# 88 instead of 80 tokens by index in a PEER trunk: sets of 64 and 24 tokens, scores and choice begun inside the query projection, a third of v in full fp32

## The chip, the cores and the metric

The kernel runs on 1 core of one Trainium2 chip. The metric is the device time of one execution in microseconds (us); one launch computes the whole output. Five engines work side by side: TensorE (PE, matmuls; its weight loads are listed apart as PEld), VectorE (DVE), ScalarE (ACT), GpSimd (POOL) and SyncE (SP), which issues most transfers; 16 DMA engines carry the transfers of all of them.

## The reference, cut to what matters

256 tokens of width 1024 go through two layers. Layer 0 mixes tokens with a convolution module, layer 1 with latent attention; after each comes a PEER block, in which every token reads 128 of 16384 experts.

```python
def peer(x, w_q, sub_keys, u, v):                      # x: 256 tokens x 1024
    q = (xt @ w_q).reshape(T, 8 heads, 2, 128)
    s = jnp.einsum('thpd,pnd->thpn', q, sub_keys)      # 128 scores, 2 sides, 8 heads
    sv, si = lax.top_k(s, 16)
    cand = sv[:, :, 0, :, None] + sv[:, :, 1, None, :]
    cv, ci = lax.top_k(cand.reshape(T, 8, 256), 16)
    experts = i1 * 128 + i2                            # 8 heads x 16 = 128 a token
    gates = jax.nn.softmax(cv)
    a = gelu(einsum('td,tkd->tk', x, u[experts])) * gates
    y = einsum('tk,tkd->td', a, v[experts])
# x = LayerNorm(alpha * x + mixer(x)), then x = LayerNorm(alpha * x + peer(x)), twice
```

u and v have 16384 rows of 4 KB each in fp32, for each layer.

## The kernel before

**Two ways through the experts.** The first DT = 176 tokens go by columns: TensorE multiplies them with all of u, in 128 blocks of 128 experts (512 KB each), ScalarE applies gelu, the result is multiplied with a sparse matrix of gates, and a second pass multiplies it with all of v, again in 128 blocks. The other SIDE = 80 tokens go by index: GpSimd fetches just their chosen rows of u and v by indirect DMAs (`gather`), one row of 4 KB to each partition, and VectorE does the sums over them (`side_dot` for u, `side_weighted` for v), 1024 elements on 128 partitions each time. The tokens by index come in sets, `SETS = ((64, 2), (16, 8))`: 64 tokens with 2 groups of partitions (64 of their rows a group), and 16 tokens with 8 groups (16 rows). That is 64 + 16 = 80 gathers of 512 KB for u and 80 for v in each layer. They have 5 rooms (`SIDE_BUFS`); gather n waits until VectorE has used the rows of n - 5 (`side_used`).

**Blocks.** SyncE loads the blocks of all weights in a fixed order into 4 rooms, and 3 more (`EXTRA`) while u and v are read; the next load waits for the room. A block is multiplied in one of two ways. *In full* (the set `FULL`): fp32 weights against fp32 tokens, which needs no other engine. *Split*: ScalarE rounds the block to fp32r (`make_high`), VectorE makes the rest (`make_low`, 1024 elements), and TensorE does 8 wide matmuls (rounded weights against both parts of the tokens side by side, 2 x DT columns) and 8 narrow ones (the rest of the weights, DT columns). In the profile a matmul in full has two records.

**Order of a layer's PEER part.** The query projection (`wq`, 16 blocks: 4 leading ones by rows, then 12 with `project_wide`; VectorE adds up the two products, `queryT`). Block 0 of u. The scores: 64 matmuls of 128 columns (32 instructions, 8 groups of four into 4 banks), copied by ScalarE. Then u's blocks up to `EARLY` = 37 without any gate, while VectorE makes the choice (`select`): 16 pairs of `top16` over the scores, 8 pairs over the candidates, then the decoding. Ahead of block `CHOSEN_AT` = 33 TensorE waits for `chosen_ok`, transposes the choice, and VectorE copies the choice of the tokens by index (`own_picks`), whereupon GpSimd starts to gather. The rest of u runs in 45 pairs of blocks (`project_merged`, `FULL_PAIRS` says which are in full); after 22 of them (`PAIR_OF`) a batch of 8 tokens is spread over the experts (`spread`, `make_onehots`, `scale_onehots`, `gate`), and `DOT_PAIRS` says which `side_dot` stands in which pair. After u come 120 blocks of v by columns (`combine_columns`; every fourth one in full, `FULL_V`), with `side_weighted` at the blocks of `SIDE_SUMS_AT` (block 4 to 113), and 8 last blocks by rows (`combine_tail`).

VectorE's order within a pair of u is: sum of the cross products, low of a coming block, the dots of `DOT_PAIRS`, the product with the gates that frees the banks (`late`), one-hots, another low, `scale_onehots`, `gate`. TensorE's next pair but one waits for `late`.

Of the kernel before, what the change touches and what calls it, by code (L numbers as in the profile page):

```python
# [14 lines left out]
P = 128  # L15
# [55 lines left out]
SET_ROWS = [PH * TOPK // _groups for _, _groups in SETS]  # L71
# [10 lines left out]
FULL_PAIRS = {1, 3, 5, 13, 21, 29, *PAIR_OF}  # L82
# [12 lines left out]
assert len(BATCH_OF) == BATCHES and len(SIDE_SUMS_AT) == SIDE_ROWS  # L95

# [32 lines left out]
FULL_V = [_n for _n in range(FIRST_COLUMNS, COLUMNS - LAST_COLUMNS) if _n % 4 == 3]  # L129
# [160 lines left out]
def program(nc, x_rows, x_cols, positions, conv_par, diag, mla_par, ln_par, keys, w_uq, w_uk, w_uv,  # L290
            u_rows, blocks, out):
    with ExitStack() as ctx:
# [213 lines left out]
        side_used = sem("side_rows_used")  # L506
        side_gelu = sem("side_hidden_made")
# [118 lines left out]
        def _(pool):  # L626
# [7 lines left out]
            nc.gpsimd.memset(rms_eps, RMS_EPS)  # L634
            nc.gpsimd.memset(ones[:], 1.0).then_inc(consts, 1)
# [23 lines left out]
            for layer in range(DEPTH):  # L659
# [5 lines left out]
                pool.wait_ge(own_picked, layer + 1)  # L665

                def fetch_picks(i, g):
                    n, rows, end_row = SETS[i][0], SET_ROWS[i], SET_ENDS[i]
                    half, at = divmod(rows * g, P // 2)
                    nc.gpsimd.dma_start(  # L670
                        picks[n * g:n * (g + 1), :, end_row - rows:end_row],
                        own_picks[SET_AT[i]:SET_AT[i] + n, :, half, at:at + rows]).then_inc(picks_in[i], 16)
# [9 lines left out]
                pool.wait_ge(picks_in[0], 16 * SETS[0][1] * (layer + 1))  # L682

                def gather(n):
                    if layer or n >= SIDE_BUFS:
                        pool.wait_ge(side_used, 2 * SIDE_ROWS * layer + max(0, n - SIDE_BUFS + 1))
                    rows, at = (u_rows, n) if n < SIDE_ROWS else (v_rows, n - SIDE_ROWS)
                    nc.gpsimd.indirect_dma_start(  # L688
                        out=side_rows[n % SIDE_BUFS], out_offset=None, in_=rows,
                        in_offset=bass.IndirectOffsetOnAxis(ap=pick_ids[:, at:at + 1], axis=0),  # L690
                        element_offset=layer * NKEYS * NKEYS * D
                    ).then_inc(side_in[n % SIDE_BUFS], 16)
                for n in range(2 * SIDE_ROWS):
# [6 lines left out]
                    elif i == 2 * groups:  # L700
                        pool.wait_ge(picks_in[1], 16 * groups * (layer + 1))
                        nc.gpsimd.memset(xT[:, :, :, DT:T].bitcast(F32), 0.0).then_inc(side_zero, 1)
# [12 lines left out]
        def _(pe):  # L715
# [180 lines left out]
            def add_sides(m):  # L896

                for pick, total in zip(selector, side_sum):
                    nc.tensor.matmul(y[:, 2 + m, :], pick, total[:, m * 512:(m + 1) * 512],  # L899
# [1457 lines left out]
```

## Time and profile before

| | |
|---|---|
| time, median of 3 runs | 1588.6 us (1587.27 to 1590.02) |
| the profiled execution: its time, its span | 1586.46 us, 1584.7 us |
| granted TensorE clock, mean | 0.998 |
| busy, share of the span | PE 98%, PEld 95%, DVE 84%, ACT 38%, POOL 38% |
| moved by DMA | 493.95 MB, mean 312 GB/s |
| layer 0: last query block ends, choice transposed, first block of v | 164.93, 250.87, 501.75 us |
| layer 1: the same | 939.75, 1025.53, 1276.83 us |

A row of a timeline is: start, length, engine, line, operation, out<-in, shape, count, and in brackets how long the engine sat idle before and what ended that. A row of windows is: stretch, its length, then for each engine the busy time and (x) instructions, the granted clock, the mean busy share of the 16 DMA engines, and GB/s moved.

### The profile page before, as it was taken

What the parts mean: (1) busy time and instruction counts of PE and PEld (TensorE: products, weight loads), DVE (VectorE), ACT (ScalarE), POOL (GpSimd) and SP (SyncE); (2) the same over time, 40 slices, a digit from 0 to 9 for tenths busy, and PEclk for the clock granted to TensorE, in tenths of its full rate; (3) what the DMA queues carried; (4) which work ended last, traced back from release to release, by engine and by line L of the source; (5) the groups of instructions that cost most, each with busy time, mean ns of one, the idle gap of its engine ahead of it and who ended that gap; (6) DMA issues with size and microseconds to landing.
All of it is one profiled execution on the core that took longest, in us unless ns stands there. A gap on an engine that the chain in (4) does not pass through costs nothing. (4 is left out here: it accounts for less than half of the span.)

```text
span 1584.7 us, 27912 instructions
## 1 busy us (share of the span) xinstructions
PE 1553.7 (98%) x10766; PEld 1497.9 (95%) x10766; DVE 1326.6 (84%) x2531; ACT 606.7 (38%) x1127; POOL 604.2 (38%) x438
## 2 busy tenths in 40 slices
PE   8999999999999999999999999999999999999998
PEld 8988999989999999999888899999999999999996
DVE  6986697889998998888856749958999988888895
ACT  5564221323234444544535341112333344444452
POOL 5651002654442555454003200046445435555420
PEclk9999999999999999999999999999999999999999
DMA  7644578999999999999823237799999999999990
GB/s 250 229 136 152 185 222 293 386 384 392 388 381 382 373 403 408 406 405 406 304 110 120 79 122 263 222 361 372 404 385 390 365 379 399 408 404 404 402 366 28
DMA packets 136964, 493.95 MB, mean 312 GB/s; under 512 B 16064, under 2 KB 16576, under 8 KB 136576
## 3 DMA queue, kind: packets, MB, share of 16 engines
q1 hardware_dynamic: 85248, 307.42, 52.4%
q0 software_dynamic: 47552, 170.06, 27.8%
q10 hardware_dynamic: 4032, 14.68, 2.6%
q8 instruction: 86, 1.41, 0.4%
q14 instruction: 46, 0.38, 0.1%
HBM read 488.79 MB, written 1.05 MB: 309 GB/s over the span
## 5 line engine op out<-in xcount | busy, mean ns | idle before, releaser
L688 POOL DMA_INDIRECT big<-v,picks x160 | 261.8, 1636 | 260.9 <-DVE big L1926 207.1
L688 POOL DMA_INDIRECT big<-u_rows,picks x160 | 214.9, 1343 | 227.6 <-DVE big L1842 193.9
L726 PE MATMUL work<-columns,raw 128*128 128x176 f32 x1728 | 268.0, 313 | 1.4 <-DVE big L1820 1.4
L726 PEld LDWEIGHTS work<-columns,raw 128*128 128x128 f32 x1728 | 259.4, 190 | 1.6 <-issue 1.6
L622 DVE TENSOR_TENSOR low<-raw,high 128x1024 fp32r<-128x1024 f32 x168 | 210.7, 1257 | 40.3 <-ACT high L1247 40.1
L1247 ACT ACTIVATE high<-raw 128x1024 fp32r<-128x1024 f32 x184 | 191.8, 1046 | 47.6 <-PE work L726 22.8
L726 PE MATMUL work<-columns,extra_raw 128*128 128x176 f32 x1280 | 202.0, 315 | 3.4 <-DVE big L1820 3.4
L1842 DVE SCALAR_TENSOR_TENSOR big<-big 128x1024 f32<-128x1024 f32 x160 | 190.2, 1218 | 15.0 <-DMA big<-u_rows,picks 15.0
L1926 DVE SCALAR_TENSOR_TENSOR big<-big,side_hid 128x1024 f32<-128x1024 f32 x156 | 199.6, 1280 | 2.3
L726 PEld LDWEIGHTS work<-columns,extra_raw 128*128 128x128 f32 x1280 | 193.5, 191 | 3.8 <-issue 3.8
L1508 ACT ACTIVATE xT<-big 128x176 fp32r<-128x176 f32 x198 | 67.6, 349 | 273.1 <-PE work L871 210.1
L866 PE MATMUL y<-xT,high 128*128 128x352 f32 x600 | 131.1, 340 | 2.4 <-DVE xT L1897 2.4
L866 PE MATMUL work<-xT,high 128*128 128x352 f32 x600 | 123.0, 326 | 0.0
L746 PE MATMUL work<-xT,high 128*128 128x352 f32 x544 | 102.8, 331 | 8.8 <-DVE big L1820 8.7
L622 DVE TENSOR_TENSOR low<-extra_raw,high 128x1024 fp32r<-128x1024 f32 x81 | 98.7, 1221 | 12.1 <-ACT high L1247 12.1
L670 POOL DMA_DIRECT2D picks<-beside_xT x20 | 12.0, 602 | 241.6 <-DVE beside_xT L1854 241.6
L866 PEld LDWEIGHTS work<-xT,high 128*128 128x128 f32 x600 | 101.0, 188 | 0.0
L866 PEld LDWEIGHTS y<-xT,high 128*128 128x128 f32 x600 | 95.9, 190 | 3.0 <-issue 3.0
L746 PEld LDWEIGHTS work<-xT,high 128*128 128x128 f32 x544 | 86.4, 188 | 11.2 <-issue 10.8
L871 PE MATMUL work<-xT,low 128*128 128x176 f32 x600 | 91.2, 274 | 0.0
L1247 ACT ACTIVATE high<-extra_raw 128x1024 fp32r<-128x1024 f32 x81 | 84.6, 1045 | 13.6 <-PE work L726 12.0
L871 PE MATMUL y<-xT,low 128*128 128x176 f32 x600 | 87.1, 267 | 0.0
(262 smaller groups left out, 2833.3 us busy)
## 6 DMA issues: line engine op xcount, KB each, us to landing
raw<-u SPq DMA_DIRECT2D x150, 512.0 KB, 6.7
raw<-v SPq DMA_DIRECT2D x146, 512.0 KB, 7.2
extra_raw<-v SPq DMA_DIRECT2D x110, 512.0 KB, 7.3
extra_raw<-u SPq DMA_DIRECT2D x106, 512.0 KB, 6.1
raw<-wq SPq DMA_DIRECT2D x32, 512.0 KB, 3.7
raw<-conv_in SPq DMA_DIRECT2D x14, 512.0 KB, 4.6
aux<-ln_par ACTq DMA_DIRECT2D x9, 512.0 KB, 9.1
raw<-conv_out SPq DMA_DIRECT2D x8, 512.0 KB, 4.0
```

What stands on the lines that cost most here:

```text
L622: ops.tensor_tensor(low_at(c), raw_at(c), high_at(c).bitcast(F32), ALU.subtract).then_inc(low_made[RAW_SLOT[c]], 1)
L670: nc.gpsimd.dma_start(picks[n * g:n * (g + 1), :, end_row - rows:end_row], own_picks[SET_AT[i]:SET_AT[i] + n, :, half, at:at + rows]).then ...
L688: nc.gpsimd.indirect_dma_start(out=side_rows[n % SIDE_BUFS], out_offset=None, in_=rows, in_offset=bass.IndirectOffsetOnAxis(ap=pick_ids[:, ...
L726: mm = nc.tensor.matmul(out_, raw_at(c)[:, k * P:(k + 1) * P], x_full[:, k, :], start=(k == 0), stop=(k == KD - 1))
L746: nc.tensor.matmul(both, w_high[:, cols], xT[:, k, :, 0:DT], start=(k == 0), stop=False)
L866: nc.tensor.matmul(columns_bank(k), high_at(c)[:, k * P:(k + 1) * P], xT[:, slot, :, 0:DT], start=start, stop=False)
L871: return nc.tensor.matmul(columns_bank(k)[:, 0, :], low_at(c)[:, k * P:(k + 1) * P], xT_high[:, slot, 0:DT], start=False, stop=stop)
L1247: A(high_at(c), raw_at(c), ACT.Copy).then_inc(high_made, 1)
L1508: A(xT_high[:, (c - v0) % KD, 0:DT], hid[:, c - v0, :], ACT.Copy).then_inc(a_high, 1)
L1842: V.scalar_tensor_tensor(rows, rows, 1.0, side_x[set_of(d)], ALU.mult, ALU.mult, accum_out=side_hid[:, d:d + 1]).then_inc(side_used, 1)
L1926: V.scalar_tensor_tensor(total, rows, weight, total, ALU.mult, ALU.add).then_inc(side_used, 1)
```

## The change

88 tokens go by index instead of 80, so 168 instead of 176 by columns. The second set has 24 tokens with 5 groups of 26 rows: 120 partitions are used, and 5 x 26 = 130 places hold 128 rows, so the picks and the hidden values are cleared once. There are 64 + 26 = 90 gathers for u and for v instead of 80; 26 of each 90 are of 120 rows. The rooms for them become 6. Six of the eight groups of score matmuls move into the query projection (after its blocks 2, 6 and 10), and VectorE takes the top 16 of six pairs there. `EARLY` goes from 37 to 29, `CHOSEN_AT` from 33 to 27; there are 49 pairs (28 in full, 21 split, before 28 and 17) and 21 batches. Of v 38 blocks instead of 29 are in full.

```diff
-EARLY = 37
+EARLY = 29
-CHOSEN_AT = 33
-EXP_AT = 24
+CHOSEN_AT = 27
+EXP_AT = 21
+SCORES_AT = (2, 6, 10)
+TOPS_AT = {4: 0, 6: 1, 8: 2, 9: 3, 10: 4, 11: 5}
-SETS = ((64, 2), (16, 8))
+SETS = ((64, 2), (24, 5))
-SET_ROWS = [PH * TOPK // _groups for _, _groups in SETS]
+SET_ROWS = [-(-PH * TOPK // _groups) for _, _groups in SETS]
+SET_USED = [_n * _groups for _n, _groups in SETS]
-FULL_PAIRS = {1, 3, 5, 13, 21, 29, *PAIR_OF}
+FULL_PAIRS = {7, 15, 21, 28, 35, 42, 47, *PAIR_OF}
-FULL_V = [_n for _n in range(FIRST_COLUMNS, COLUMNS - LAST_COLUMNS) if _n % 4 == 3]
+FULL_V = [_n for _n in range(FIRST_COLUMNS, COLUMNS - LAST_COLUMNS) if _n % 3 == 1]
...
                 def gather(n):
...
                     rows, at = (u_rows, n) if n < SIDE_ROWS else (v_rows, n - SIDE_ROWS)
+                    used = SET_USED[set_of(at)]
                     nc.gpsimd.indirect_dma_start(
-                        out=side_rows[n % SIDE_BUFS], out_offset=None, in_=rows,
-                        in_offset=bass.IndirectOffsetOnAxis(ap=pick_ids[:, at:at + 1], axis=0),
+                        out=side_rows[n % SIDE_BUFS][0:used], out_offset=None, in_=rows,
+                        in_offset=bass.IndirectOffsetOnAxis(ap=pick_ids[0:used, at:at + 1], axis=0),
...
-                for c in range(FIRST[wq] + LEAD[wq] + HALVES, end_of[wq]):
+                full = FIRST[wq] + LEAD[wq]
+                for c in range(full + HALVES, end_of[wq]):
                     project_wide(wq, c)
+                    if c - full == SCORES_AT[0]:
+                        pe.wait_ge(lead_ok, HALVES * (layer + 1))
+                        pe.wait_ge(keys_in, 16 * (layer + 1))
+                        make_scores(0, 2)
+                    elif c - full == SCORES_AT[1]:
+                        pe.wait_ge(emptied, PROJECTED[wq] + 4)
+                        make_scores(2, 4)
+                    elif c - full == SCORES_AT[2]:
+                        pe.wait_ge(emptied, PROJECTED[wq] + 8)
+                        make_scores(4, 6)
...
                 pe.wait_ge(emptied, PROJECTED[f"u{layer}"])
...
+                make_scores(6, 8)
                 project(f"u{layer}", 1, CHOSEN_AT)
...
+            def top_pair(layer, pair):
+
+                n = pair // 2
+                j = HP * (n % HALVES) + 4 * (n // HALVES) + 2 * (pair % 2)
+                dve.wait_ge(score_ok, 8 * layer + n + 1)
+                top16([(j + lane, scores[:, j + lane, :], rest[lane]) for lane in range(2)], top_v, top_u)
+
             def select(layer):
 
-                dve.wait_ge(score_ok, 8 * (layer + 1))
...
+                for pair in range(len(TOPS_AT), HP):
+                    top_pair(layer, pair)
...
                     make_low(dve, V, c + RING)
+                    if c - full in TOPS_AT:
+                        top_pair(layer, TOPS_AT[c - full])
                 select(layer)
```

**TensorE, from the last query blocks to the transposed choice.** `work<-xT` with 512 columns is a wide query matmul, `y<-big 128x128` a score matmul, `work<-columns` a block of u in full (x8 is one block), `y<-ident,aux` the choice transposed. Before:

```order
L807 MATMUL work<-xT,high 128x512 x8
L810 MATMUL work<-xT,low 128x256 x8
L726 MATMUL work<-columns,raw 128x176 x8
L1154 MATMUL y<-big 128x128 x32
L726 MATMUL work<-columns,raw 128x176 x24
```

and the same place in the changed kernel:

```order
L826 MATMUL work<-xT,high 128x512 x8
L829 MATMUL work<-xT,low 128x256 x8
L1167 MATMUL y<-big 128x128 x8
L826 MATMUL work<-xT,high 128x512 x8
L829 MATMUL work<-xT,low 128x256 x8
L745 MATMUL work<-columns,raw 128x168 x8
L1167 MATMUL y<-big 128x128 x8
L745 MATMUL work<-columns,raw 128x168 x24
```

Of the 32 score matmuls 24 have moved ahead of u, in three pieces of 8, the last of which is the first `y<-big` shown here; 8 stay behind u's block 0.

**GpSimd, the gathers of layer 0.** `big<-u_rows,picks` and `big<-v,picks` are gathers of u and of v, `picks<-beside_xT` brings a part of the choice. Before, from the last piece of the second set's tokens on:

```order
L676 DMA big<-x 16x1024
L688 DMA big<-u_rows,picks 128x1024
L702 MEMSET xT 128x16x80
L688 DMA big<-u_rows,picks 128x1024 x55
L688 DMA big<-v,picks 128x1024 x80
```

and in the changed kernel:

```order
L694 DMA big<-x 24x1024
L707 DMA big<-u_rows,picks 128x1024
L721 MEMSET xT 128x16x88
L707 DMA big<-u_rows,picks 128x1024 x45
L707 DMA big<-u_rows,picks 120x1024 x26
L707 DMA big<-v,picks 128x1024 x64
L707 DMA big<-v,picks 120x1024 x26
```

The second set's gathers are of 120 rows now, and there are 26 of them instead of 16, for u and for v.

## Rows read from the trace of the kernel before

**Rows 1.** The page, busy times and bandwidth in 40 slices
```profile
PE 1553.7 (98%) x10766; PEld 1497.9 (95%) x10766; DVE 1326.6 (84%) x2531; ACT 606.7 (38%) x1127; POOL 604.2 (38%) x438
...
GB/s 250 229 136 152 185 222 293 386 384 392 388 381 382 373 403 408 406 405 406 304 110 120 79 122 263 222 361 372 404 385 390 365 379 399 408 404 404 402 366 28
```

**Rows 2.** Windows: the stretches of gathers, and parts of the first
```profile
257.50:755.30 497.80, 490.41 (x3638) 487.40 (x3637) 442.15 (x597) 189.94 (x343) 248.30 (x177) 1.00 1.01 391
300.00:340.00 40.00, 37.00 (x282) 36.22 (x282) 33.63 (x53) 12.40 (x26) 26.29 (x26) 1.00 1.03 376
340.00:360.00 20.00, 19.91 (x158) 19.66 (x158) 19.93 (x30) 6.31 (x13) 10.04 (x7) 1.00 1.03 406
...
580.00:600.00 20.00, 20.00 (x145) 20.00 (x145) 19.01 (x24) 9.01 (x15) 10.97 (x7) 1.00 1.03 409
...
1033.00:1528.00 495.00, 488.27 (x3616) 485.75 (x3616) 433.55 (x574) 186.30 (x337) 248.63 (x177) 1.00 1.01 391
```

**Rows 3.** DMA issues: KB each, us from issue to landing
```profile
raw<-v SPq DMA_DIRECT2D x146, 512.0 KB, 7.2
...
raw<-wq SPq DMA_DIRECT2D x32, 512.0 KB, 3.7
...
big<-u_rows,picks POOLq DMA_INDIRECT x160, 8.4
```

**Rows 4.** Timeline of PE: blocks of u, in full and split
```profile
486.72 2.55 PE L726 MATMUL work<-columns,raw 128*128 128x176 f32 x16
489.10 1.06 PE L1181 MATMUL y<-aux 128*128 128x128 f16 x16
490.02 1.54 PE L746 MATMUL work<-xT,high 128*128 128x352 f32 x8
491.40 1.03 PE L749 MATMUL work<-xT,low 128*128 128x176 f32 x8
492.26 1.50 PE L746 MATMUL work<-xT,high 128*128 128x352 f32 x8
```

**Rows 5.** Timeline of PE: blocks of v, one round of four
```profile
508.90 1.39 PE L879 MATMUL y<-big,extra_raw 128*128 128x176 f32 x8
...
515.68 0.84 PE L866 MATMUL y<-xT,high 128*128 128x352 f32 x4
...
517.87 1.39 PE L879 MATMUL y<-big,extra_raw 128*128 128x176 f32 x8
```

**Rows 6.** Timeline of PE: last query block to the transposed choice
```profile
162.13 2.00 PE L807 MATMUL work<-xT,high 128*128 128x512 f32 x8
...
164.93 2.55 PE L726 MATMUL work<-columns,raw 128*128 128x176 f32 x16
167.32 7.31 PE L1154 MATMUL y<-big 128*128 128x128 f32 x64
174.46 7.33 PE L726 MATMUL work<-columns,raw 128*128 128x176 f32 x48
...
250.87 0.88 PE L1165 MATMUL y<-ident,aux 128*128 128x128 f32 x6
```

**Rows 7.** Timeline of DVE: last query sum, first pairs of the choice
```profile
165.54 0.42 DVE L2221 TENSOR_TENSOR big<-work,cross 128x256 f32<-128x256 f32 x1 [2.37 <-ACT cross L1478]
175.29 0.49 DVE L1698 MAX8 big<-big 128x8 f32<-128x128 f32 x2 [9.32 <-ACT big L1484]
...
177.65 0.47 DVE L1698 MAX8 big<-big 128x8 f32<-128x128 f32 x2
```

**Rows 8.** Timeline of POOL: the first gather of layer 0
```profile
257.47 1.17 POOL L688 DMA_INDIRECT big<-u_rows,picks  x1 [3.39 <-DMA picks<-beside_xT]
```

**Rows 9.** Groups of DVE by line, 256 to 502 us
```profile
L1842 DVE SCALAR_TENSOR_TENSOR big<-big 128x1024 f32<-128x1024 f32 x80 | 95.0, 1218 | 7.2 <-DMA big<-u_rows,picks 7.2
...
L622 DVE TENSOR_TENSOR low<-raw,high 128x1024 fp32r<-128x1024 f32 x22 | 26.8, 1219 | 4.3 <-ACT high L1247 4.3
...
L1820 DVE TENSOR_TENSOR big<-work,big 128x16 f32<-128x16 f32 (+21 forms) x44 | 15.1, 344 | 14.6 <-ACT work L1498 14.6
```

More of the change, by code:

```diff
@@ L95, with pick_pieces @@
 assert len(BATCH_OF) == BATCHES and len(SIDE_SUMS_AT) == SIDE_ROWS
+def pick_pieces(i, g):
+    lo, hi = SET_ROWS[i] * g, min(SET_ROWS[i] * (g + 1), PH * TOPK)
+    return [(a, b) for a, b in ((lo, min(hi, P // 2)), (max(lo, P // 2), hi)) if a < b]
+PICK_LOADS = [sum(len(pick_pieces(_i, _g)) for _g in range(SETS[_i][1])) for _i in range(len(SETS))]
 def set_of(d):
@@ L506, in program @@
         side_used = sem("side_rows_used")
+        side_filled = sem("side_tables_zeroed")
         side_gelu = sem("side_hidden_made")
@@ L681, in _ @@
                     fetch_tokens(0, g)
-                pool.wait_ge(picks_in[0], 16 * SETS[0][1] * (layer + 1))
+                pool.wait_ge(picks_in[0], 16 * PICK_LOADS[0] * (layer + 1))
                 def gather(n):
@@ L700, in _ @@
                     elif i == 2 * groups:
-                        pool.wait_ge(picks_in[1], 16 * groups * (layer + 1))
+                        pool.wait_ge(picks_in[1], 16 * PICK_LOADS[1] * (layer + 1))
                         nc.gpsimd.memset(xT[:, :, :, DT:T].bitcast(F32), 0.0).then_inc(side_zero, 1)
@@ L896, in add_sides @@
             def add_sides(m):
-                for pick, total in zip(selector, side_sum):
-                    nc.tensor.matmul(y[:, 2 + m, :], pick, total[:, m * 512:(m + 1) * 512],
+                for pick, total, used in zip(selector, side_sum, SET_USED):
+                    nc.tensor.matmul(y[:, 2 + m, :], pick[0:used], total[0:used, m * 512:(m + 1) * 512],
                                      start=False, stop=False)
@@ L1471, in _, with copy_scores @@
                         highs_to(full + RING)
+                def copy_scores(lo, hi):
+                    for n in range(lo, hi):
+                        at = HP * (n % HALVES) + 4 * (n // HALVES)
+                        act.wait_ge(score_mm, 8 * layer + n + 1)
+                        A(scores[:, at:at + 4, :].rearrange("p j n -> p (j n)"), y[:, n % 4, :],
+                          ACT.Copy).then_inc(score_ok, 1)
                 for c in range(full, end_of[wq]):
@@ L1479, in _ @@
                     highs_to(c + RING)
+                    if n - 1 in SCORES_AT:
+                        copy_scores(2 * SCORES_AT.index(n - 1), 2 * SCORES_AT.index(n - 1) + 2)
                 u0 = FIRST[f"u{layer}"]
-                for n in range(HALVES * HP // 4):
-                    act.wait_ge(score_mm, 8 * layer + n + 1)
-                    A(scores[:, 4 * n:4 * n + 4, :].rearrange("p j n -> p (j n)"), y[:, n % 4, :],
-                      ACT.Copy).then_inc(score_ok, 1)
+                copy_scores(6, 8)
                 def gelu(n):
```

80 lines of the change are left out of this document (42 added, 38 removed).

## The prediction

> **What bounds the kernel now.** First the page: TensorE is busy for 98% of the span, and nearly the same slices that hold u and v move 380 to 408 GB/s and never more [rows 1]. So there are two candidates, TensorE and the DMA engines, and I looked at whether either has room. From the first gather of layer 0 (257.5 us) to the 113th block of v (755.3 us) TensorE works for 490.4 of 497.8 us, so it waits for 7.4 us, at the full clock; VectorE works for 442 of them; and the DMA engines have a mean busy share of 1.01 while they move 391 GB/s. Layer 1 repeats it: 391 GB/s over 495 us [rows 2]. A share of 1.01 means that each of the 16 engines has a packet under way all the time. The pieces of that stretch show where it tops out: 409 GB/s from 580 to 600 us, 406 from 340 to 360, and 376 from 300 to 340, where the small pieces of the choice are moved too, all with a share of 1.03 [rows 2]. A load of a block takes 3.7 us alone and 7.2 us in this stretch, a gather 8.4 [rows 3]: they queue. So TensorE sets the pace today, with the DMA engines at 391 of some 404 GB/s right behind it: 3% of room. VectorE is the third: in u it carries 80 dots of 1.19 us (95.0 / 80), and TensorE's few stalls come through its line L1820, which waited 14.6 us for gelus [rows 9].
>
> The chance of a gain lies where TensorE sets the pace; a change that asks for more bytes in less time must pass the other limit.
>
> **What TensorE saves.** A block of u in full starts 2.38 us before what follows (486.72 to 489.10), a split one takes 2.24 us: 1.38 us for 8 wide matmuls and 0.86 for 8 narrow ones; a batch's spread takes 0.92 [rows 4]. In v one round of four blocks takes 8.97 us, a split block in it 2.19 (515.68 to 517.87) [rows 5]. A block in full has 16 records of 176 columns in 2.38 us, 149 ns each, which is 2 x 176 columns at 2.4 GHz (147 ns) and 2 ns; with 168 columns it is 142 ns or 2.28 us. A wide matmul loses 16 columns, 6.7 ns, so a split block 0.05 us. The narrow ones take 108 ns at 176 columns where the columns alone would be 73; something else sets that, so I take nothing for them (at most 8 x 3.3 ns, 0.03 us). In v a third in full makes a round of three 2.28 + 2 x 2.15 = 6.58 us, 2.19 a block instead of 2.24.
>
> After the choice u has before 61 blocks in full, 34 split and 22 spreads: 145.2 + 76.2 + 20.2 = 241.6 us, and took 250.9 (250.87 to 501.75 in the table). After the change: 59 in full, 42 split, 21 spreads: 134.5 + 92.0 + 19.3 = 245.8. To block 113 of v: 113 x 2.24 = 253.1 before, 247.5 after. TensorE alone would thus need 493 us from the choice on, where it took 504.
>
> **When the choice comes.** Before, the last query block ends at 164.93, u's block 0 and 7.14 us of scores follow (167.32 to 174.46), then 32 blocks; TensorE arrives at 250.87 and waits for nothing [rows 6]. VectorE starts its first pair at 175.29, after 9.32 us of idling, and needs 2.36 us a pair [rows 7], so 16 pairs last to 212.9; the rest (to 250.8) is 37.9. After: six of eight groups of scores, 5.4 us, lie in the projection, which then ends at 170.3. A block takes 2.80 us there (162.13 to 164.93 [rows 6]), and VectorE has 0.42 for its sum [rows 7] and 1.22 for a low [rows 9]; three pairs stand at blocks with a low, where it falls behind by about 1.2 us and catches up at the next block without a pair; the other three at blocks without one. So I cost these at nothing; if TensorE did wait there, it would be 1.2 us at each of three places. The last sum ends at 171.3, pair 5 and ten more follow without a pause: 25.9, then 37.9: 235.1. TensorE gets there at 170.3 + 27 x 2.28 + 1.8 = 233.7 and waits 1 us or so. The choice comes at 234.9, 16.0 us earlier. The first gather keeps its distance (257.47, 6.6 us behind the transposition [rows 8]), and 6 more blocks of u are yet to be loaded and multiplied.
>
> **VectorE in u.** 10 more dots (11.9 us), 8 more lows (9.8), 4 more cross sums and products with gates (some 3), one batch less (3.3): about 21 us more on top of the roughly 218 it works between 256 and 502 us. That is 239 in a stretch of some 255; it is near the limit but does not exceed what the transfers need (below). In v 10 more sums of 1.28 stand against 9 lows and 9 small operations less: nothing.
>
> **What the DMA engines must carry.** The stretch of rows 2 moved 497.8 us x 391 GB/s = 194.6 MB, that is 371 transfers of 512 KB. The change adds: 20 gathers, of which 52 of now 180 are 120 / 128 of a whole: 16.75 transfers; 6 blocks that were there already when gathers started: 6. It takes away the lead that blocks have at the end: with 7 rooms at 2.24 us a block a room comes round every 15.7 us, of which 7.2 is the load [rows 3] and 2.2 the multiplication, so about 3 blocks lie ready; in a stretch that the transfers limit they are used up: -3. The sum is +19.75 transfers, 10.4 MB, 205.0 MB in all. What rate? The low bound is that of before over the whole stretch, 391; the high bound is 409 everywhere. With work queued all the time the idle moments go, while the small pieces of the choice (376 for 40 us) stay; a stretch of 40 us at 376 and the rest at 404 to 409 is 404 to 406. I take 402, since VectorE near its limit will leave some gaps. 205.0 / 0.402 = 510 us, 12 more than before; less 16.0 for the earlier choice: -4 us a layer. TensorE's 493 us, 6.6 of it before the first gather, are hidden under these 510 + 6.6.
>
> Outside of this stretch the change touches 7 blocks of v (0.3 us) and two clears of GpSimd at the start: nothing. Two layers: -8 us. The profiled execution's 1586.5 us becomes 1578.5 (its span 1584.7 becomes 1577); it lies 2.1 us under the median of the runs, so the forecast is 1581 us.
>
> Where that turns: the rate at which the longer list takes exactly 497.8 + 16.0 us is 399 GB/s. Above, the change is faster, below, slower. At 391 it is 524 us: +10.5 a layer. At 406 it is 505: -9.
>
> One price is not in the trace: a gather of 120 rows. From the rows it costs between 120/128 of a whole one (taken) and a whole one, if the engines that hold most rows set its end: 52 / 16 = 3.25 transfers more, +4.2 us a layer, and the forecast becomes no change. The Trainium skill (DMA: Bandwidth & Descriptors, section Queues, rings and completion order) says that a transfer is split over the largest number of engines up to 16 that divides the partitions, 15 for 120, taken in turn, and that some direct copies by GpSimd put the partitions divided by 16, rounded up, on each engine, which would be 8 on each of the first 15. By the first way the smaller price holds, by the second the larger; no run so far shows which.
>
> **The rivals.**
>
> *TensorE keeps the pace.* If the engines could carry what is asked, each layer would take 16.0 us less up to the choice and 504 - 493 = 11 less behind it, or 2 less if the same stalls stay: -18 to -27 a layer, 1535 to 1553 us, middle 1544. For it: TensorE's 98%. Against it: v would ask for a block each 2.19 us and a gather each 1.233 blocks, 524 KB x (1 / 2.19 + 1 / 2.70) = 433 GB/s, and no window with a share of 1.03 is above 409 [rows 2]. The same page (section Specifications) gives a ceiling of 435 GB/s for the core's ports. By that rule this rival holds, and the time is its 1544 us; the trace, at 409 with every engine busy, speaks against it. Chance 0.12.
>
> *The transfers take more than they give.* The stretch keeps its rate of 391, since bursts of gathers and full rooms leave the same gaps, or VectorE's 239 us of work and late gathers hold each other up in u: +10.5 us a layer, 1610 us; with whole-price gathers up to 1618. It decides from under 399 GB/s. For it: the stretches of both layers had a share of 1.01 already and still only 391. Against: the 7.4 us in which TensorE waited show that before it was not the transfers that were asked for all they could. Chance 0.28, its smaller sizes (1592 up) included.
>
> *It cancels.* 399 GB/s, or 402 with gathers at the whole price: 1585 to 1592 us. Chance 0.18.
>
> My forecast, the transfers set the pace at 400 to 406 GB/s, 1568 to 1585 us, has 0.42.
>
> **The numbers.** The likeliest alone spans 1568 to 1585. The range must take in the cancelling and most of the slower case: 1558 to 1607; about 0.1 is left out on each side. A change of up to 0.2% (3.2 us) is about what a measurement of this kernel can't tell from none. Faster than that: 0.12 and 0.40 of the forecast's case, 0.52. Within: 0.17. Slower: 0.31.
>
> **What the changed profile would show.** DMA at a share of 1.03 and 400 to 409 GB/s all through both stretches; TensorE's records in full at 142 ns; TensorE busy for clearly less than 98% there, with waits that end at lows of late blocks or at gathers, in v too, where it had none; loads of v landing after more than 7.2 us. The choice transposed near 235 us. If TensorE works without gaps in v at 2.19 us a block, I am wrong about the ceiling; if the rate stays near 391 with gaps in the share, the slower case holds; if the choice comes later than 236 us, VectorE was held up in the projection. First block of v near 492 to 496 us in layer 0.

## The result and the profile after

The changed kernel takes 1734.3 us (median of 4 runs, 1731.8 to 1739.8) where the kernel before takes 1588.8 beside it: a ratio of 1.0922 (95% interval 1.0907 to 1.0937), 145.5 us slower. The forecast was 1581, and the slowest rival ended at 1618. The profiled execution of the changed kernel took 1733.2 us, its span is 1731.4.

First the page of the changed kernel, the lines that answer to [rows 1] and the chain of waits with its largest entries:

```profile
PE 1574.2 (91%) x10734; PEld 1498.0 (87%) x10734; DVE 1363.5 (79%) x2581; ACT 603.2 (35%) x1113; POOL 638.4 (37%) x470
...
DMA  7544789999999999999833247999999999999991
GB/s 245 194 139 145 246 294 374 408 409 337 272 271 370 406 408 408 346 269 276 296 125 122 93 168 245 356 373 408 408 288 276 328 374 409 409 408 296 280 282 55
DMA packets 142564, 511.46 MB, mean 295 GB/s; under 512 B 17392, under 2 KB 17904, under 8 KB 142176
...
DMA 16%; PE 6%; DVE 2%; ACT 1%; issue 1%; SPq 0%; DVEq 0%; ACTq 0%
```

TensorE's work barely grew (1574 against 1554 us), but it fills 91% of the span instead of 98%. The bandwidth is what to look at. It has four holes, each two to four slices wide, in which it falls from 408 to some 270 to 280 GB/s, while the line above it says that the DMA engines are busy for 90% or more of those slices. The chain of waits, followed back from the end, now goes through transfers.

Where the holes lie in time, from the windows of the changed kernel (columns as in [rows 2]). The fence starts with two pieces of good stretches and one hole in u and one in v of layer 0, then all of the stretch; the last four rows are the second sets of gathers, from their first gather to their last (u and v of layer 0, u and v of layer 1):

```profile
380.00:400.00 20.00, 20.00 (x163) 19.91 (x163) 18.52 (x28) 6.20 (x15) 9.85 (x9) 1.00 1.03 408
440.00:480.00 40.00, 31.18 (x218) 30.72 (x219) 30.51 (x46) 9.93 (x23) 17.04 (x12) 0.91 1.03 273
600.00:660.00 60.00, 58.07 (x412) 56.14 (x412) 51.61 (x63) 23.48 (x35) 30.96 (x22) 1.00 1.03 408
720.00:760.00 40.00, 29.13 (x174) 27.78 (x173) 19.12 (x23) 9.14 (x14) 10.07 (x9) 0.87 1.03 273
241.00:765.00 524.00, 471.11 (x3421) 461.62 (x3421) 423.78 (x580) 171.93 (x315) 246.17 (x180) 0.96 1.02 360
...
414.00:508.00 94.00, 75.59 (x538) 73.85 (x537) 68.09 (x100) 20.41 (x48) 35.67 (x26) 0.91 1.02 270
711.00:817.00 106.00, 80.01 (x500) 76.89 (x499) 60.47 (x68) 26.80 (x40) 34.55 (x26) 0.90 1.03 279
1263.00:1355.00 92.00, 74.74 (x542) 72.82 (x541) 68.96 (x102) 20.64 (x50) 36.01 (x28) 0.92 1.02 272
1560.00:1661.00 101.00, 76.30 (x506) 72.55 (x504) 60.37 (x67) 26.73 (x40) 34.18 (x26) 0.96 1.03 282
```

Two columns matter. The share of the DMA engines is 1.03 in the good stretches and in the holes alike: they never lack work. But the same share moves 408 GB/s in the one and 273 in the other, so a packet takes longer. Its time can be worked out from a row, as nearly all bytes go in packets of 4 KB: 16 engines x 1.03 x 4096 B / 408 GB/s = 165 ns, and 247 ns at 273 GB/s. The trace has each packet with its queue and says the same of both. From 440 to 480 us a packet of 4 KB takes 246 ns on average on GpSimd's queue and 243 on SyncE's, from 600 to 660 us 163 and 164; nine in ten take over 210 ns in the hole, nine in ten at most 169 in the good stretch. The page bears it out for SyncE's queue (packets, MB, share of the 16 engines' span), before and after:

```profile
q1 hardware_dynamic: 85248, 307.42, 52.4%
```

```profile
q1 hardware_dynamic: 85248, 307.42, 51.8%
```

These are the same packets, in 16 x 0.524 x 1584.7 us before, 156 ns each, and in 16 x 0.518 x 1731.4 us after, 168 ns each over the whole execution. The holes begin and end with the 26 gathers of 120 rows. The four rows together last 393 us at a mean of 276 GB/s; at 408 the same bytes would have needed 266 us. That is 127 of the 145.5 us, read from the trace alone; whether the shape of the gathers is the cause, only runs can say.

The granted clock, the third column from the right, is 0.87 to 0.96 in the holes, so TensorE spent a part of them at its lower level, 1.2 GHz, after it had sat idle. It still sat idle for 11 of 40 us at 0.87, so I take the clock for a result of the hole and not for what sets its length; experiment 2 has the same rates at a clock of 1.00.

What the engines wait for in the changed kernel (in total, times, longest):

```profile
DVE low L635 <- ACT high L1279: 176.5, 115, 10.1
ACT high L1279 <- DMA extra_raw<-v: 112.0, 63, 7.0
...
PE work L765 <- DVE big L1863: 43.6, 19, 7.2
...
ACT high L1279 <- DMA raw<-v: 34.8, 23, 3.7
PE y L885 <- DVE low L635: 32.2, 43, 3.2
ACT high L1279 <- DMA raw<-u: 30.2, 9, 12.3
```

ScalarE waits for loads of v and u that SyncE issued, not only for gathers: the holes slow both queues. VectorE's lows wait for ScalarE, TensorE for VectorE.

The choice did come early. TensorE's timeline in the changed kernel, where it answers to [rows 6]:

```profile
227.78 3.01 PE L745 MATMUL work<-columns,raw 128*128 128x168 f32 x20
230.63 4.72 PE L745 MATMUL work<-columns,extra_raw 128*128 128x168 f32 x32
235.97 0.88 PE L1197 MATMUL y<-ident,aux 128*128 128x128 f32 x6 [0.61 <-DVE aux L1810]
```

It is transposed at 235.97 us, 14.9 us earlier than before, after a wait of TensorE of 0.6 us; 20 records in full take 2.85 us, 142.5 ns each.

### The profile page after: what moved, and what is told of

It is laid out like the page before. It is cut to its first block and busy times, and to the rows that moved or that the text cites. A ratio compares the mean times of both kernels' runs of the same rounds, so it can differ in the third digit from the quotient of the medians.

```text
span 1731.4 us, 27963 instructions
## 1 busy us (share of the span) xinstructions
PE 1574.2 (91%) x10734; PEld 1498.0 (87%) x10734; DVE 1363.5 (79%) x2581; ACT 603.2 (35%) x1113; POOL 638.4 (37%) x470
## 2 busy tenths in 40 slices
DMA packets 142564, 511.46 MB, mean 295 GB/s; under 512 B 17392, under 2 KB 17904, under 8 KB 142176
## 5 line engine op out<-in xcount | busy, mean ns | idle before, releaser
L745 PE MATMUL work<-columns,raw 128*128 128x168 f32 x1568 | 240.9, 312 | 15.1 <-DVE big L1863 11.5
L1886 DVE SCALAR_TENSOR_TENSOR big<-big 128x1024 f32<-128x1024 f32 (+1 forms) x180 | 213.8, 1218 | 22.0 <-DMA big<-u_rows,picks 22.0
L1972 DVE SCALAR_TENSOR_TENSOR big<-big,side_hid 128x1024 f32<-128x1024 f32 (+1 forms) x176 | 225.1, 1279 | 4.3
L745 PE MATMUL work<-columns,extra_raw 128*128 128x168 f32 x1184 | 183.0, 311 | 11.7 <-DVE big L1863 9.6
L765 PE MATMUL work<-xT,high 128*128 128x336 f32 x672 | 131.8, 341 | 43.6 <-DVE big L1863 43.6
L885 PE MATMUL y<-xT,high 128*128 128x336 f32 x536 | 118.2, 343 | 42.6 <-DVE low L635 32.2
L1547 ACT ACTIVATE xT<-big 128x168 fp32r<-128x168 f32 x180 | 59.0, 336 | 160.5 <-PE work L890 151.9
L885 PE MATMUL work<-xT,high 128*128 128x336 f32 x536 | 106.8, 321 | 0.0
L898 PE MATMUL y<-big,raw 128*128 128x168 f32 x544 | 94.2, 318 | 0.0
L768 PE MATMUL work<-xT,low 128*128 128x168 f32 x672 | 91.9, 283 | 0.0
L768 PEld LDWEIGHTS work<-xT,low 128*128 128x128 f32 x672 | 91.6, 204 | 0.0
```

The costliest lines, as they stand in the source:

```text
L745: mm = nc.tensor.matmul(out_, raw_at(c)[:, k * P:(k + 1) * P], x_full[:, k, :], start=(k == 0), stop=(k == KD - 1))
L765: nc.tensor.matmul(both, w_high[:, cols], xT[:, k, :, 0:DT], start=(k == 0), stop=False)
L768: mm = nc.tensor.matmul(both[:, 0, :], w_low[:, cols], xT_high[:, k, 0:DT], start=False, stop=(k == KD - 1))
L885: nc.tensor.matmul(columns_bank(k), high_at(c)[:, k * P:(k + 1) * P], xT[:, slot, :, 0:DT], start=start, stop=False)
L898: mm = nc.tensor.matmul(columns_bank(k)[:, 0, :], raw_at(c)[:, k * P:(k + 1) * P], hid[:, n, :], start=False, stop=False)
L1547: A(xT_high[:, (c - v0) % KD, 0:DT], hid[:, c - v0, :], ACT.Copy).then_inc(a_high, 1)
```

## The experiments

The theories after this reading. **A:** a gather that does not cover the 128 partitions slows every packet that flies beside it. **B:** something else in the change does it (six rooms, the order of the loads, the early choice, VectorE), and the gathers of 120 rows only happen to be there.

### 1. The gathers of 120 rows, taken out and put in

The changed kernel with its second set's gathers over all 128 partitions (the last 8 fetch rows that nobody uses):

```diff
-                        out=side_rows[n % SIDE_BUFS][0:used], out_offset=None, in_=rows,
-                        in_offset=bass.IndirectOffsetOnAxis(ap=pick_ids[0:used, at:at + 1], axis=0),
+                        out=side_rows[n % SIDE_BUFS], out_offset=None, in_=rows,
+                        in_offset=bass.IndirectOffsetOnAxis(ap=pick_ids[:, at:at + 1], axis=0),
```

> The changed kernel, with one difference: the gathers of the second set run over all 128 partitions (the 8 unused ones fetch row 0), and VectorE still works on 120 of them. Theory A, the shape of 120 partitions slows every packet that is under way beside it: no stretch falls to 270 GB/s, all stay at 376 to 409, and the time comes back to where the forecast had put it with gathers at the whole price, 1580 to 1605 us. Theory B, the second set's stretches are slow for another reason (its tokens, its places in the program, VectorE's load, TensorE's half clock): they stay at about 270 GB/s and the time stays at 1730 us.

Measured: 1605.1 us (1602.8 to 1611.0), ratio 1.0122 (1.0097 to 1.0146), the upper end of what theory A had put. It moves 3.4 MB more (514.86 against 511.46) and is 129.2 us faster: 1.24 us for each of the 104 gathers. Its windows:

```profile
300.00:340.00 40.00, 37.04 (x280) 36.57 (x281) 38.07 (x59) 12.48 (x27) 20.14 (x15) 0.96 1.03 409
340.00:400.00 60.00, 58.02 (x468) 57.58 (x468) 56.22 (x87) 19.41 (x44) 29.21 (x21) 1.00 1.02 406
400.00:440.00 40.00, 37.14 (x286) 36.61 (x284) 37.17 (x55) 12.58 (x30) 20.44 (x16) 0.96 0.98 376
440.00:480.00 40.00, 38.01 (x302) 37.48 (x300) 39.09 (x56) 12.69 (x29) 19.16 (x15) 1.00 1.00 388
...
560.00:760.00 200.00, 192.98 (x1368) 187.15 (x1367) 168.03 (x192) 79.38 (x118) 103.41 (x68) 1.00 1.03 407
...
241.00:765.00 524.00, 500.33 (x3738) 491.15 (x3738) 462.67 (x624) 191.29 (x343) 268.33 (x192) 0.99 1.02 398
```

The holes are gone: 388 GB/s where 273 stood, and 407 through v. Theory A holds for nine tenths of the loss. A rest of 17 us stays; experiment 3 is about it.

The other way round: the kernel before, and nothing changed in it but that the last 16 gathers of each pass are of 120 rows, and in a second run of 112.

```diff
+                    used = P if at < SET_ENDS[0] else 120
-                        out=side_rows[n % SIDE_BUFS], out_offset=None, in_=rows,
-                        in_offset=bass.IndirectOffsetOnAxis(ap=pick_ids[:, at:at + 1], axis=0),
+                        out=side_rows[n % SIDE_BUFS][0:used], out_offset=None, in_=rows,
+                        in_offset=bass.IndirectOffsetOnAxis(ap=pick_ids[0:used, at:at + 1], axis=0),
```

> The kernel before, with its last 16 gathers of each pass (of 80) cut to 120 of 128 partitions; the last 8 partitions keep rows of earlier gathers, so a part of the sums of 16 tokens is of other experts. Fewer bytes are moved. Theory A: each of the four stretches of 16 such gathers (some 50 us at 404 GB/s) needs 1.5 times as long for its bytes, less the 3% of room: about 20 us each, 1660 to 1680 us. Theory B: nothing changes, 1588 us.

> The same with 112 partitions, 7 for each of 16 DMA engines; 16 partitions keep rows of earlier gathers, so a part of the sums of 16 tokens is of other experts. If what harms is that 120 does not divide by 16 (theory A1), this runs at the pace of before, 1585 to 1589 us. If every gather of fewer than 128 partitions harms (A2), it is 1660 us or more, as with 120.

Measured: with 120 rows 1653.8 us (1651.2 to 1659.3), ratio 1.0428 (1.0407 to 1.0449), though it moves 2.1 MB less than the kernel before; 66 us for 64 gathers, 1.03 us each. That is less than the 1.24 of the changed kernel, perhaps because that one had no room left in its transfers, and it lies 6 us under the 1660 to 1680 expected. With 112 rows 1625.5 us (one run), 38 us, 0.59 each: between the two expectations (1585 to 1589, and 1660 or more), so both missed, and harm is there all the same. Windows of the first of the two, a good stretch of v and the two holes of layer 0:

```profile
440.00:480.00 40.00, 34.54 (x250) 33.96 (x249) 34.78 (x48) 10.85 (x24) 14.82 (x13) 0.91 1.03 285
...
660.00:700.00 40.00, 40.00 (x288) 40.00 (x287) 35.07 (x41) 19.12 (x30) 21.39 (x13) 1.00 1.03 404
720.00:760.00 40.00, 33.31 (x209) 32.51 (x208) 24.51 (x29) 13.38 (x21) 10.59 (x9) 0.91 1.03 285
```

Neither the early choice nor the sixth room is in this kernel, and the holes are. Theory B is out for the main loss. 112 is a multiple of 16 and does harm as well, so it takes no number of rows that 16 does not divide.

### 2. The rate by itself

A kernel of transfers alone, in phases of 30: 4 KB a row, gathers on GpSimd's queue, loads of blocks on SyncE's, six rooms each.

```python
PHASES = [("g128", ((0, 128),), 0), ("g120", ((0, 120),), 0), ("g112", ((0, 112),), 0), ("g96", ((0, 96),), 0),
...
          ("load128", (), 128), ("load120", (), 120),
          ("g128 load128", ((0, 128),), 128), ("g120 load128", ((0, 120),), 128),
```

> Transfers alone, no computation (the output is zeros): phases of 30 gathers of u's rows over 128, 120, 112, 96, 64 partitions, over 64 + 56 and over 112 + 8 in two pieces; 30 loads of 128 and of 120 partitions; then gathers of 128, 120, 112, 64 + 56 partitions with 30 loads of 128 beside them. Rates at 128: about 405 GB/s. Theory A1: 120 partitions bring the rate to some 270 GB/s, with and without loads beside them, with packets of 240 ns instead of 165; 112, 96 and 64 + 56 stay near 400. If 120 alone runs at 380 or more and falls only beside loads, the harm lies in the mixture: gather packets and load packets that meet at the same partitions.

Its windows; the columns after the length are VectorE, GpSimd, the clock, the share and GB/s. In order: gathers of 128 rows, of 120, of 112, of 96; loads of 128 rows, of 120; gathers of 128 with loads of 128; gathers of 120 with loads of 128:

```profile
10.00:40.00 30.00, 0.00 (x0) 21.84 (x24) 1.00 1.02 414
50.00:100.00 50.00, 0.00 (x0) 25.35 (x27) 1.00 1.03 271
110.00:160.00 50.00, 0.00 (x0) 23.15 (x25) 1.00 1.03 249
170.00:210.00 40.00, 0.00 (x0) 22.16 (x25) 1.00 1.03 251
412.00:445.00 33.00, 0.00 (x0) 0.00 (x0) 1.00 1.02 416
455.00:510.00 55.00, 0.00 (x0) 0.00 (x0) 1.00 0.97 235
520.00:585.00 65.00, 0.00 (x0) 23.07 (x25) 1.00 1.03 420
600.00:695.00 95.00, 0.00 (x0) 23.34 (x24) 1.00 1.03 284
```

The whole effect is here with no compute engine at work: 414 GB/s against 271 for gathers, and a plain load that SyncE issues shows it too, 416 against 235. So it needs neither the indirect addressing nor GpSimd's queue. In the last two rows the loads are the same and only the gathers beside them shrink by 8 rows: 420 falls to 284, with the engines always busy. That is the hole of the kernel (273), and the 285 of the experiment before. The expectation that 112, 96 and 64 + 56 rows stay near 400 GB/s was wrong: they moved 249, 251 and 202. In that last phase each full set of rows goes in two pieces, and the share was only 0.73; 112 + 8 rows did no better (202 at 0.72), and 64 rows moved at 211. Beside loads, gathers of 112 rows left 306 GB/s where those of 120 left 284, in the order of their prices in the kernel before, 0.59 and 1.03 us.

The Trainium skill (SBUF — State Buffer, section Door 1: The DMA port swizzle) says that the rate depends on how many of the 16 ports of SBUF the partitions reach, and its last section, Summary: rules for kernel authors, advises 128 partitions and one transfer instead of several where the transfers are the bound. The trace agrees with the advice: 414 against 271, 249 and 251 GB/s, and 202 for two pieces. It does not agree with the count of ports as the reason: by the page's map partitions 0 to 95 reach all 16 already, and 96 rows moved at 251. Whether the engines get in each other's way at the ports was not tried here, nor whether reading or writing is what slows, and the mechanism stays open.

A second kernel of this kind asks how few and how small such transfers may be:

```diff
+PHASES = [("g128 load128", ((128,), ()), 128),
+          ("g128 g128 g120 load128", ((128, 128, 120), ()), 128),
+          ("g124 load128", ((124,), ()), 128),
+          ("g128 and rows 0 to 16 load128", ((128,), ((0, 16),)), 128),
+          ("g128 and rows 112 to 128 load128", ((128,), ((112, 128),)), 128),
+          ("g128 and rows 0 to 64 load128", ((128,), ((0, 64),)), 128),
+          ("load 64 and 64", ((), ()), 64),
+          ("load 32 four times", ((), ()), 32)]
```

> Transfers alone, in phases of 30 rounds (the output is zeros, nothing is computed); a gather of 128 rows of 4 KB on GpSimd's queue and a load of 128 rows on SyncE's queue in each round, and beside them what the phase says. (1) nothing more: 420 GB/s, 159 ns a packet, as measured. (2) every third gather of 120 rows: by theory A (any transfer that does not span the 128 partitions slows what flies beside it) 340 to 380 GB/s; by theory B (only a queue full of such gathers does) 415. (3) all gathers of 124 rows: A about 285 as with 120; B 400 or more. (4, 5) a load of 16 rows more in each round, at partitions 0 to 15 and at 112 to 127: A 350 to 400 GB/s; B 415 or more. (6) a load of 64 rows more: A 300 to 370. (7) only loads, each of 128 rows cut in two of 64: A 210 to 300, B 410. (8) cut in four of 32: A 200 to 250. Phases 4 and 5 say whether the small loads of picks and tokens explain why three sets were 9 us slower than two although they move less.

Its windows, one in each phase, in the order of the list:

```profile
20.00:60.00 40.00, 0.00 (x0) 15.03 (x16) 1.00 1.03 420
100.00:160.00 60.00, 0.00 (x0) 18.37 (x20) 1.00 1.03 336
180.00:240.00 60.00, 0.00 (x0) 10.07 (x8) 1.00 1.05 256
340.00:400.00 60.00, 0.00 (x0) 25.37 (x34) 1.00 1.03 356
440.00:500.00 60.00, 0.00 (x0) 24.74 (x34) 1.00 1.03 355
540.00:600.00 60.00, 0.00 (x0) 20.04 (x26) 1.00 1.03 337
660.00:700.00 40.00, 0.00 (x0) 0.00 (x0) 1.00 1.03 243
740.00:780.00 40.00, 0.00 (x0) 0.00 (x0) 1.00 1.04 235
```

One gather of 120 rows in three, so one such transfer in six, already costs 20% (336 of 420). 64 KB more in each round, to 16 partitions, cost 15%, wherever they go (356 at partitions 0 to 15, 355 at 112 to 127). A block cut in two halves of 64 partitions moves at 243 GB/s. Five of the numbers lie within what theory A had put; one gather in three (336 for 340 to 380) and 124 rows (256 for about 285) lie under it, and none is near theory B. The 256 is no mixture of equal parts: from 180 to 240 us the trace has 2868 load packets of 4 KB and only 883 of gathers. Once the loads were through, the gathers of 124 rows alone moved 156 to 187 GB/s (260 to 320 us).

### 3. The other 17 us, and the forecast's own question

With whole gathers the rest of the change can be seen: is it then bound by the transfers, as the prediction had it? The first of these kernels takes away bytes alone: every fifth gather fetches 512 B a row.

```diff
+                    width = D
+                    if at % 5 == 4:
+                        width, rows = D // 8, u_eighths if n < SIDE_ROWS else v_eighths
-                        out=side_rows[n % SIDE_BUFS], out_offset=None, in_=rows,
+                        out=side_rows[n % SIDE_BUFS][:, 0:width], out_offset=None, in_=rows,
```

> The changed kernel with all gathers over 128 partitions, and every fifth one of u and of v fetching 512 B a row instead of 4 KB (left out: the sums over those 36 gathers a layer use what else stands in the room). No engine does less, only the DMA engines: 16.5 MB less a layer, 33 MB in all. Theory A (with whole gathers 88 tokens are bound by the transfers, 398 GB/s from the choice to the end of v): up to 16.5 MB / 398 GB/s = 41 us less a layer, cut off where TensorE alone takes over, at 493 instead of 524 us: 1540 to 1570 us. Theory B (TensorE, or its waits for VectorE, set the pace, and the transfers only fill the time): 1595 to 1605 us, the GB/s falling instead by 6%.

Measured: 1566.2 us (1563.5 to 1570.5), ratio 0.9863 (0.9846 to 0.9880): 39 us less than with whole gathers, for 33.0 MB less (481.83 against 514.86), so 1.18 us a MB or 19.5 us a layer. With whole gathers the transfers are a bound, and the time lies in what theory A had put. They do not stay one for long: 33.0 MB at 398 GB/s are 83 us, and only 39 came back before something else took over. Its windows, in u and in v:

```profile
440.00:480.00 40.00, 37.10 (x294) 36.57 (x294) 39.12 (x60) 12.74 (x31) 20.60 (x15) 1.00 0.97 361
...
600.00:660.00 60.00, 60.00 (x444) 60.00 (x442) 52.98 (x60) 25.83 (x40) 34.01 (x22) 1.00 1.02 404
```

In this part of v TensorE now works without a gap, 60.00 of 60 us. In u it does not: 37.1 of 40, and the third of the busy times shows VectorE at 39.1 of 40.

The second: three sets without an unused place, 64 + 16 + 8 tokens, 88 gathers instead of 90.

```diff
-SETS = ((64, 2), (24, 5))
+SETS = ((64, 2), (16, 8), (8, 16))
```

> 88 tokens by index in three sets, 64 in 2 groups, 16 in 8 and 8 in 16: 64 + 16 + 8 = 88 gathers for u and for v in each layer, all of 128 rows and none with a place unused, instead of 64 + 26 = 90. The rest is the changed kernel. Against the run with whole gathers (1605 us) it moves 4 x 0.524 = 2.1 MB a layer less and VectorE has 4 passes of about 1.2 us less. Theory A (bound by the transfers at 398 GB/s): 5.3 us a layer less, 1592 to 1597 us, so still slower than the kernel before. Theory B (TensorE sets the pace): 1603 to 1606 us.

Measured: 1614.1 us (1609.6 to 1619.3), ratio 1.0160 (1.0139 to 1.0182). Both theories missed. By the medians it is 9 us slower than with two sets, by the ratios 6, and the two intervals just meet (1.0139 and 1.0146); what is sure is that the gain of 10 us did not come. The windows where the picks and tokens of the two small sets are fetched:

```profile
300.00:340.00 40.00, 36.30 (x285) 35.51 (x284) 34.85 (x54) 13.07 (x29) 29.09 (x26) 1.00 1.03 385
340.00:400.00 60.00, 56.62 (x458) 55.70 (x457) 55.80 (x85) 19.04 (x42) 43.00 (x42) 1.00 1.03 387
```

385 and 387 GB/s, where two sets had 409 and 406, at the same share. Those fetches are transfers to 16 and to 8 partitions, 48 a layer instead of a dozen; experiment 2 shows that a load of 16 rows of 4 KB takes 15% off the rate. The loads of tokens are of that kind, the picks are not, and the trace keeps them apart: 408 GB/s while the 16-token set's picks are fetched (261 to 282 us) and 370 while its tokens are (283 to 305); for the 8-token set 395 and 385 (307 to 352, 353 to 396). With two sets it is 403 (260 to 280) and 343 (280 to 300, five loads of 24 rows). Over 100 us a layer 5% is 5 us, as much as the 2.1 MB gave back, so this would account for a gain of nothing instead of 5.3 us a layer; it was not tried by itself, and the whole stretch moves 396 GB/s in layer 0 and 387 in layer 1, where two sets moved 398 and 395. Some 3 or 4 us a layer more are not accounted for; this kernel also has 5 rooms for gathers instead of 6, and VectorE's wait for gathers of u rose from 14 to 24 us in all. Which of these it is was not tried.

The third: whole gathers, and every fourth block of v in full again.

```diff
-FULL_V = [_n for _n in range(FIRST_COLUMNS, COLUMNS - LAST_COLUMNS) if _n % 3 == 1]
+FULL_V = [_n for _n in range(FIRST_COLUMNS, COLUMNS - LAST_COLUMNS) if _n % 4 == 3]
```

> 88 tokens, all gathers over 128 partitions, and v as before, every fourth block in full instead of every third. At 80 tokens the same edit gave 4.6 us (1586.4 to 1581.8). Theory A (88 tokens are bound by the transfers): nothing to be had, 1603 to 1607 us, as the run with whole gathers. Theory B (TensorE sets the pace of v here too): 4 us less, 1601 us or under.

Measured: 1601.4 us (1598.8 to 1610.0), ratio 1.0100 (1.0074 to 1.0127), whose interval overlaps that of the third in full. The time lies between the two theories, next to B's 1601. The profile speaks for A: the same 407 GB/s in v, TensorE working 192.7 of 200 us against 193.0, and of the 4.0 us between the profiled executions 2.3 are there where v of layer 0 starts (500.2 against 502.5), in code that they share. I count this as unresolved.

### 4. The rest of the change at 80 tokens

The old sets in the changed kernel, which brings its 5 rooms back; and on top of that v with every fourth block in full, and with every sixth.

```diff
-SETS = ((64, 2), (24, 5))
+SETS = ((64, 2), (16, 8))
```

> The changed kernel with the old sets: 64 tokens in 2 groups and 16 in 8, so 80 tokens by index and every gather 128 rows. The rest of the change stays (scores and the first top 16 within the query projection, the choice at block 27, 49 pairs, a third of v in full). The bytes are those of the kernel before. Theory A (the whole loss is the gathers of 120 rows and the bytes of 10 gathers more; the rest of the change is harmless): the time of before or a little under, 1578 to 1590 us, the transfers 390 to 400 GB/s from the first gather on, the choice transposed near 237 us. Theory B (the early choice or the longer work of VectorE in u costs time of its own): 1595 us or more.

> The same kernel (80 tokens, all gathers of 128 rows, the early choice), but v as before, every fourth block in full. Against the run with a third of v in full it tells who sets the pace of v at 80 tokens. Theory A (TensorE sets it): 9 blocks a layer at 2.24 us split instead of 2.38 in full, 1.3 us a layer, so 2 to 3 us faster than the run with the third, 1576 to 1588 us. Theory B (the transfers set it, or VectorE does, which gets 9 more blocks of 0.6 us a layer to make low): the same within 1 us, or some us slower than with the third.

> The fastest version so far (80 tokens, early choice, a quarter of v in full, 1581.8 us), with every sixth block of v in full instead of every fourth, so 10 blocks a layer fewer in full. Theory A (TensorE sets the pace of v and VectorE has room, 53 of 60 us busy): by 4.6 us for 18 blocks, 0.26 us a block, 5 us less: 1576 to 1579 us. Theory B (VectorE becomes the bound, 10 more blocks of 1.2 us to make low in 260 us of v, and one wait for it shows): 1582 us or more.

Measured: a third in full 1586.4 us (1584.5 to 1588.6, 11 runs), ratio 0.9984 (0.9975 to 0.9992); a quarter 1581.8 (1578.5 to 1585.4), ratio 0.9956 (0.9943 to 0.9969); a sixth 1583.1 (1582.2 to 1589.8, 10 runs), ratio 0.9975 (0.9964 to 0.9987), as theory B of that run had it. So the early choice and the new order of u are worth 0.4%, 6.6 us, a third of v in full gives back 4.6 of them (2 to 3 were expected), and the version with a quarter beats both kernels. Its windows in u and v of layer 0, and behind them the same two of the kernel with a sixth of v in full:

```profile
241.00:500.00 259.00, 251.84 (x1930) 249.56 (x1930) 237.78 (x346) 92.07 (x189) 128.81 (x101) 0.99 0.99 372
...
560.00:760.00 200.00, 200.00 (x1429) 200.00 (x1427) 178.47 (x208) 92.16 (x140) 99.71 (x61) 1.00 1.02 403
```

```profile
241.00:500.00 259.00, 252.11 (x1946) 249.96 (x1945) 239.12 (x349) 94.17 (x195) 127.10 (x101) 0.99 1.00 376
...
560.00:760.00 200.00, 199.77 (x1433) 199.42 (x1432) 188.89 (x225) 102.88 (x158) 107.84 (x61) 1.00 1.02 403
```

At 80 tokens TensorE works without a gap in v, so a block less in full is a gain, as long as VectorE has room. With a sixth VectorE works for 188.9 of 200 us instead of 178.5, and TensorE, at 199.77, has its first gaps in v; nothing more is gained. The intervals of the quarter and the sixth overlap, so the best point lies between them or at the quarter.

## Why the prediction was wrong

**The step that failed is the price of a gather of 120 rows.** It was put between 120/128 of a whole one and a whole one, 0 to 4.2 us a layer. Measured, it costs 1.24 us more than a whole one (129.2 us / 104), which itself is worth 0.524 MB / 399 GB/s = 1.31 us. That makes it about two whole gathers, and 52 of them a layer cost 65 us beyond the upper of the two prices. The error is in what was priced. I asked how long such a transfer keeps the engines that it uses, and took the packets to stay as they were. They don't: the packets of both queues, SyncE's loads too, go from some 165 to some 245 ns while it is under way. The sentence before the price was right that the trace did not show it; the bounds then came from counts of rows in a transfer, not from a rate that a row shows. There was such a row: from 300 to 340 us, "where the small pieces of the choice are moved too", the kernel before moved 376 GB/s at a share of 1.03, against 409 [rows 2]. I took those pieces as bytes that cost their time. Most of them are the eight loads of 16 rows of tokens (305 to 324 us), and packets of 4 KB take 177 ns in those 40 us, on either queue, against 163 from 580 to 600. Read as small transfers beside which all others are slower, the row would have given a rival with 52 such transfers a layer. No sign that the prediction lists is a rate that falls at a full share.

**The two ways of sharing out rows** that the prediction took from the Trainium skill (DMA: Bandwidth & Descriptors) stand there in the section Why a DMA increments its semaphore by 16 and not by 1, not in the one that it names. They decided between two small prices, and neither holds a word of the packets' time. That 15 engines carry 120 rows, the trace may bear out: the loads of 120 rows had a share of 0.97 where whole ones had 1.02, and gathers of them, whose engines would change in turn, 1.03. It is worth 6%, and the loss was a third.

**The choice** came at 235.97 us for a forecast of 234.9, and TensorE waited 0.6 us for a forecast of 1: right within 1.1 us.

**The times of TensorE's blocks** were right: 142.5 ns a record in full for 142.

**The ceiling** was right for this kernel: 408 to 409 GB/s in its good stretches, and in no window of 20 us or more above 410, though transfers alone reached 420. So the rival in which TensorE keeps the pace was rightly held small for this change. With 6.4% of the bytes taken out the time was 1566 us and still not that rival's 1544. What holds it there was not tried; in u VectorE was busy for 39.1 of 40 us.

**The rate of 402 GB/s and the sum.** Without the failed step the measured kernel is that with whole gathers, 1605 us: the rival in which the transfers take more than they give, at 0.28, not the forecast. In v the rate was 407, above the 402 taken; in u, from 400 to 480 us, 376 and 388 with a share of 0.98 and 1.00, where VectorE worked for 37.2 and 39.1 of 40 us. The prediction's own mixture, 40 us at 376 and the rest at 404 to 409, gives 402 to 406, not 404 to 406, so that 402 had no gap in it. "It is near the limit but does not exceed what the transfers need" was too favourable by that. VectorE, forecast at 239 us in 255, worked for 231 in 253 (242 to 495 us); that it left these gaps is read from the windows, not tried. The mean over 241 to 765 us was 398 GB/s, 1 under the turning rate of 399, and in layer 1 (1015 to 1540 us) 395. With whole gathers 205.0 MB become 206.7, at 398 GB/s 519 us and at 395 523; less the 16.0, that is 5.5 and 9.5 us longer than the 497.8 of before. The two layers make 15 us, and measured were 17 (1605.1 - 1588). So the sum was right within 1 or 2 us a layer once rate and price are put right, and the sign hung on 1% of rate.

**VectorE in v and the shape of v.** "A third in full" was costed as 2.19 us a block instead of 2.24 with 168 columns. At 176 columns it costs 4.6 us in the whole kernel against a quarter, 0.26 us for each of the 18 blocks. The rows of v give 8.97 - 3 x 2.19 = 2.40 us for the block in full, 0.21 more than a split one; the prediction took 2.28 - 2.15 = 0.13 with 168 columns, because its price of a block in full came from u. The sign was right, the size half. At 88 tokens with whole gathers the difference was not resolved.

## What to carry to other kernels

Where transfers run near their ceiling, give every one of them all 128 partitions, even if some rows are fetched for nothing: here the 8 spare rows were 6% of a gather, and leaving them out cost about a second gather. A share of busy DMA engines says that they have work, not that they move it; look at GB/s beside the share, and where the rate falls at a full share, look for the shape of what is in flight. When two limits lie within 3% of each other, a change that feeds one by loading the other has its sign in the third digit of a rate, and the low end of that rate belongs in the forecast.

## What the runs showed of the hardware

- A transfer over fewer than 128 partitions slows the packets beside it, on both queues (246 and 243 ns for 163 and 164): gathers of 120, 112 and 96 rows alone 271, 249 and 251 GB/s for 414; loads of 120 rows 235 for 416; loads of 128 rows with gathers of 120 beside them 284 for 420, of 112 306, and 256 with fewer gathers, of 124 rows, beside them. Why is open.
- It takes few of them: one in six transfers, 336 GB/s; a load of 16 rows for each two whole ones, 356; blocks in halves of 64 partitions, 243, in quarters of 32, 235.
- Transfers alone reach 420 GB/s on one core; in the kernels no window of 20 us or more was above 410.
- TensorE's granted clock fell to a mean of 0.87 of its upper level in stretches where it sat idle for 11 of 40 us.
